# A two-block transformer kernel on Trainium2: the second norm summed per token, two query splits moved ahead, and the expert lists made between slabs 32 and 40

## The reference, cut to what matters

```python
h2 = modulate(x, norm2_g[l], shift2, scale2)          # rms_norm(x) * g * (1 + scale) + shift
q = (hf @ w_q).reshape(t, 8, 256)                     # PEER: 8 heads
s1, s2 = q[..., :128] @ keys_1.T, q[..., 128:] @ keys_2.T
v1, i1 = top_k(s1, 16); v2, i2 = top_k(s2, 16)
sc, ci = top_k(all 256 sums v1 + v2, 16)              # 16 experts per head of 16384
gates = softmax(sc)
a = gelu(einsum('td,ted->te', hb, u_tab[eb]))
out = einsum('te,ted->td', gates * a, v_tab[eb])
```

## Time and profile before

| What | Value |
|---|---|
| median of 3 runs | 1734.45 us (1734.1 to 1734.72) |
| the profiled execution's own time | 1732.42 us |
| its span | 1730.7 us |
| TensorE busy | 1639.6 us, 95% of the span |
| VectorE busy | 1067.3 us, 62% |
| ScalarE busy | 851.8 us, 49% |
| GpSimd busy | 492.4 us, 28% |
| mean granted TensorE clock | 0.974 |
| second norm, queries | about 184 to 264 us |
| slabs 0 to 39 | 266 to 387 us |
| lists, first gated slab | 387 to 398 us |

### The profile page before, as it was taken

How to read it: one execution, slowest core, us unless ns; L and a number is a source line. 1 busy time by engine, 2 the same in 40 slices (tenths; PEclk the granted TensorE clock), 3 DMA queues, 4 the chain that set the end, 5 groups by cost and what they waited for, 6 DMA issues and landing times.

```text
span 1730.7 us, 33796 instructions
## 1 busy us (share of the span) xinstructions
PE 1639.6 (95%) x11134; PEld 1490.6 (86%) x11134; DVE 1067.3 (62%) x2463; ACT 851.8 (49%) x1806; POOL 492.4 (28%) x485
## 2 busy tenths in 40 slices
PE   6998599999999999999999999889999999899998
PEld 4778598999999999887788877779999988789997
DVE  5665479907777751455565555866555665765555
ACT  3433345654444444555555553455555535754554
POOL 3110597885666678200000002411000000410000
PEclk9997799999999999999999999899999999999999
DMA  8871244553444445555555554227555435045554
GB/s 336 292 251 66 99 158 147 182 181 113 144 135 144 134 151 182 188 188 190 193 194 187 191 192 152 70 77 265 182 182 182 149 107 183 13 159 176 188 186 154
DMA packets 81330, 288.19 MB, mean 167 GB/s; under 512 B 10144, under 2 KB 11472, under 8 KB 81136
## 3 DMA queue, kind: packets, MB, share of 16 engines
q1 hardware_dynamic: 71296, 253.11, 44.0%
q0 software_dynamic: 8640, 31.07, 4.9%
q10 hardware_dynamic: 1328, 3.15, 0.5%
HBM read 284.66 MB, written 2.62 MB: 166 GB/s over the span
## 4 chain that ended last, share of the span: by engine, by line
PE 82%; DVE 7%; POOL 5%; issue 3%; ACT 3%; DMA 1%; DVEq 0%; ACTq 0%; POOLq 0%; SPq 0%
PE pu L615 12%; PE pu L616 11%; PE pu L617 11%; PE pacc L672 8%; PE pacc L674 8%; PE pacc L673 8%; POOL ring_lo L397 3%; PE pu L583 3%; PE pu L595 2%; PE pacc L615 2%; PE pacc L617 2%; PE pacc L616 2%; PE pn L960 2%; PE pm L960 2%; PE pacc L732 1%
## 5 line engine op out<-in xcount | busy, mean ns | idle before, releaser
L390 ACT ACTIVATE ring_hi<-ring 128x512 fp32r<-128x512 f32 x896 | 515.0, 622 | 545.8 <-PE pu L617 304.9
L397 DVE TENSOR_TENSOR ring_lo<-ring,ring_hi 128x512 fp32r<-128x512 f32 x608 | 395.9, 693 | 329.0 <-ACT ring_hi L390 328.8
L615 PE MATMUL pu<-Xh,ring_hi 128*128 128x256 f32 x1472 | 433.1, 294 | 33.5 <-POOL ring_lo L397 19.4
L616 PE MATMUL pu<-Xl,ring_hi 128*128 128x256 f32 x1472 | 421.4, 286 | 0.0
L617 PE MATMUL pu<-Xh,ring_lo 128*128 128x256 f32 x1472 | 421.2, 286 | 0.0
L397 POOL TENSOR_TENSOR ring_lo<-ring,ring_hi 128x512 fp32r<-128x512 f32 x288 | 370.2, 1307 | 131.9 <-ACT ring_hi L390 113.6
L615 PEld LDWEIGHTS pu<-Xh,ring_hi 128*128 128x128 f32 x1472 | 287.2, 195 | 40.6 <-issue 32.8
L616 PEld LDWEIGHTS pu<-Xl,ring_hi 128*128 128x128 f32 x1472 | 287.7, 195 | 0.2
L617 PEld LDWEIGHTS pu<-Xh,ring_lo 128*128 128x128 f32 x1472 | 286.9, 195 | 0.0
L674 PE MATMUL pacc<-ring_lo,vh 128*128 128x512 f32 x512 | 200.6, 392 | 0.0
L672 PE MATMUL pacc<-ring_hi,vh 128*128 128x512 f32 x512 | 200.5, 392 | 0.0
(11 more groups left out here) (402 smaller groups left out, 2649.4 us busy)
## 6 DMA issues: line engine op xcount, KB each, us to landing
ring<-in_weights SPq DMA_DIRECT2D x480, 512.0 KB, 3.4
big<-in_ada POOLq DMA_DIRECT2D x40, 512.0 KB, 6.4
big<-in_w1k POOLq DMA_DIRECT2D x8, 512.0 KB, 8.9
bias_row<-big ACTq DMA_DIRECT2D x1, 1536.0 KB, 6.8
XT<-in_xT ACTq DMA_DIRECT2D x1, 1024.0 KB, 8.4
scr<-in_ada POOLq DMA_DIRECT2D x2, 512.0 KB, 12.4
tk<-in_ada POOLq DMA_DIRECT2D x2, 512.0 KB, 14.1
early_h<-in_ada POOLq DMA_DIRECT2D x2, 512.0 KB, 16.1
```

Of the source, the lines that this page charges most:

```text
L390: nc.scalar.activation(ring_hi[:, n % 2, half], ring[:, n % RING, half], ACT.Copy).then_inc(s["split_hi"], 1)
L397: api.tensor_tensor(ring_lo[:, n % RING, half], ring[:, n % RING, half], ring_hi[:, n % 2, half], ALU.subtract).then_inc(s[LOW[name][0]], 1)
L615: mm(out, ring_hi[:, n % 2, w], xh, start=start, stop=False, skip_group_check=True)
L616: mm(out, ring_hi[:, n % 2, w], xl, start=False, stop=False, skip_group_check=True)
```

## The change

Three edits, all in the first block.

1. **The second norm.** GpSimd no longer adds squares. TensorE multiplies each chunk's squares (as the stationary side, one 128x128 block per half of the tokens) by one column of ones, so the sums come out with tokens on partitions, two columns in all. The sums of chunks 0 to 3 come before `out_slot(7)`, those of 4 and 5 after it, those of 6 and 7 after the last squares. Root and reciprocal work on two columns, and two products with the identity (an operand that repeats one column) spread the inverse roots to a 128x256 tile in PSUM, which `h2_scale` reads.
2. **The first query splits.** GpSimd makes the low parts of query tiles 0 and 1 right after its nine memsets; the loop behind the wait for `ada_used` has tiles 2 to 15, with one of the 14 memsets after each.
3. **The lists.** The loop of ungated slabs ends at 32. Slabs 32 to 39 are written out: the exponent comes after slab 31, the transposes after slab 34 on TensorE, the copies after the gelu of slab 35 on ScalarE. VectorE gets a wait for slab 39's result before its first `combine`.

```diff
+LISTS_AT = 32
             for k in range(mid_lo, mid_hi, 4):
                 step(nc.gpsimd.memset(big[:, k:min(k + 4, mid_hi), :], 1.0))
-            pool.wait_ge(s["h2_sq"], 2)
-            h2sum = R[:, T:2 * T]
-            step(nc.gpsimd.tensor_tensor(h2sum, sq[:, 0, :], sq[:, 1, :], ALU.add))
-            for c in range(2, C - 2):
-                pool.wait_ge(s["h2_sq"], c + 1)
-                last = nc.gpsimd.tensor_tensor(h2sum, h2sum, sq[:, c, :], ALU.add)
-                if c < C - 3:
-                    step(last)
-            last.then_inc(s["h2_sum"], 1)
+            split_low(pool, nc.gpsimd, "peer_q", 0)
+            split_low(pool, nc.gpsimd, "peer_q", 1)
...
-            for i in range(2 * PH):
+            for i in range(2, 2 * PH):
                 split_low(pool, nc.gpsimd, "peer_q", i)
-                for lo, hi in parts[i::2 * PH]:
+                for lo, hi in parts[i - 2::2 * PH - 2]:
                     step(nc.gpsimd.memset(big[:, lo:hi, :], 1.0))
...
-            for i in range(2, 8):
+            def h2_sums(c):
+                for tt in range(TT):
+                    last = mm(paccf[:, tt * 512:tt * 512 + 1], sq[:, c, tt * P:(tt + 1) * P], ones[:, 0:1],
+                              start=(c == 0), stop=(c == C - 1), skip_group_check=True)
+                return last
+            for i in range(2, 7):
                 out_slot(i)
+            for c in range(4):
+                pe.wait_ge(s["h2_sq"], c + 1)
+                h2_sums(c)
+            out_slot(7)
+            for c in range(4, C - 2):
+                pe.wait_ge(s["h2_sq"], c + 1)
+                h2_sums(c)
+            pe.wait_ge(s["squares"], SQUARED["n2"])
+            h2_sums(C - 2)
+            h2_sums(C - 1).then_inc(s["sums"], 1)
             pe.wait_ge(s["normed"], NORM["gla"])
-            pe.wait_ge(s["h2_sum"], 1)
-            mm(pn[:, 0:T], ones[:, :], R[:, T:2 * T], start=True, stop=False)
-            pe.wait_ge(s["squares"], SQUARED["n2"])
-            mm(pn[:, 0:T], ones[:, :], sq[:, C - 2, :], start=False, stop=False)
-            mm(pn[:, 0:T], ones[:, :], sq[:, C - 1, :], start=False, stop=True).then_inc(s["sums"], 1)
+            pe.wait_ge(s["inverses"], 4)
+            for tt in range(TT):
+                last = mm(pn[:, tt * P:(tt + 1) * P], over_columns(R[:, tt:tt + 1]), ident[:, :], start=True, stop=True)
+            last.then_inc(s["spreads"], 1)
...
-            with pe.Fori(0, GATED_FROM // BODY) as g:
+            with pe.Fori(0, LISTS_AT // BODY) as g:
...
-            pe.wait_ge(s["lists_ready"], 1)
-            (six transposes, lists_psum)
+            for k in range(LISTS_AT, GATED_FROM):
+                up_slot("peer_u", k, USE["peer_u"] + k, None, 0)
+                if k == LISTS_AT + 2:
+                    pe.wait_ge(s["lists_ready"], 1)
+                    for tt in range(TT):
+                        for q in range(3):
+                            bank = (pm, pn)[tt]
+                            last = nc.tensor.transpose(bank[:, q * P:(q + 1) * P], tk[:, 1536 + (q * TT + tt) * P:
+                                                       1536 + (q * TT + tt + 1) * P], ident[:, :])
+                    last.then_inc(s["lists_psum"], 1)
...
-            root(NORM["n2"])
+            act.wait_ge(s["sums"], NORM["n2"])
+            f(R[:, 0:TT].rearrange("p (a b) -> p a b", b=1),
+              paccf[:, 0:TT * 512].rearrange("p (a b) -> p a b", b=512)[:, :, 0:1],
+              ACT.Sqrt, scale=1.0 / D, bias=eps[:, 0:1]).then_inc(s["roots"], 1)
...
-            act.wait_ge(s["lists_psum"], 1)
...
+            for k in range(LISTS_AT, GATED_FROM):
+                split_high(act, "peer_u", k + 2)
+                expert_tile(k)
+                if k == LISTS_AT + 3:
+                    act.wait_ge(s["lists_psum"], 1)
+                    for tt in range(TT):
+                        last = f(Rl[:, :, tt * P:(tt + 1) * P],
+                                 (pm, pn)[tt][:, 0:3 * P].rearrange("p (q t) -> p q t", q=3), ACT.Copy)
+                    last.then_inc(s["lists_copied"], 1)
...
-                v.scalar_tensor_tensor(HTf[:, c, :], XT[:, c, :], gain[:, 8 + c:9 + c], R[:, 0:T], ALU.mult, ALU.mult)\
+                v.scalar_tensor_tensor(HTf[:, c, :], XT[:, c, :], gain[:, 8 + c:9 + c], pn[:, 0:T], ALU.mult, ALU.mult)\
...
-            step(v.reciprocal(R[:, 0:T], R[:, 0:T]))
+            v.reciprocal(R[:, 0:TT], R[:, 0:TT]).then_inc(s["inverses"], 1)
+            dve.wait_ge(s["spreads"], 4)
...
+            dve.wait_ge(s["evacs"], USE["peer_u"] + GATED_FROM)
             with dve.Fori(GATED_FROM // BODY, (GATED_FROM + GROUPS) // BODY - 1) as g:
```

More of the change, by code:

```diff
@@ L118 @@
 NSA_OUT = OUTNO[SPAN["nsa"][0]]
-SEMS = """c_loaded x_loaded cols_loaded relb_loaded small_loaded xn_ready h_scaled h_chunks h2_sq h2_sum h2_scaled h2_hi h2_lo consts_made casts_made c_silu ada_used chain_dve chain_act chain_pool slots_used evacs alr_psum
+SEMS = """c_loaded x_loaded cols_loaded relb_loaded small_loaded xn_ready h_scaled h_chunks h2_sq h2_scaled h2_hi h2_lo consts_made casts_made c_silu ada_used chain_dve chain_act chain_pool slots_used evacs alr_psum
 alr_copied z_psum squares sums roots normed la_parts ex_ready ex_done silu_done gla_ops kl_psum kl_copied gla_scores
@@ L1477, in _ @@
             split_high(act, "peer_u", 1)
-            with act.Fori(0, GATED_FROM // BODY) as g:
+            with act.Fori(0, LISTS_AT // BODY) as g:
                 for k in range(BODY):
```

## The result

The changed kernel takes **1715.78 us** (median of 4 runs, 1715.42 to 1716.95), against 1734.3 for the kernel before beside it (1734.1 to 1734.72): a ratio of 0.9894, 95% interval 0.9877 to 0.9911. The forecast was 1716.8, in a range of 1712 to 1723. The profiled execution took 1715.42 us, with a span of 1713.5.

What follows compares the result with a forecast made beforehand. The prediction took TensorE to bound the kernel, so only its waits or lower-clock time could pay. 11.1 us at the queries (norm included) plus 6.6 at the lists gave 17.7, from 1734.45 to 1716.8, range 1712 to 1723.

Steps and rivals of the forecast that it cites:

- The norm: Second norm: first scaling at 189.9 instead of 193.46, 3.6 us earlier, or 2.2 if both TensorE steps are slow.
- The first queries: Query tiles: first query at 191.4 instead of 206.59, but tile 15 gains only 11.1 us, paced by GpSimd's 3.48-us rounds.
- Rival 1, the half clock: Query tiles: TensorE stays at 1.2 GHz beyond tile 1, each tile taking 2.7 us more; chance 0.08 mild, 0.03 full.
- mild: Half clock for two query tiles: 5.4 us less 2.1 of slack, 1720.1; chance 0.08.
- full: Half clock for all 14 query tiles: tile 15 starts 33.0 us after the forecast, 1752 in all; chance 0.03.
- The sign that I had named: Query tiles: the granted clock at 0.5 past 204 would show the forecast wrong.
- the slack: Query tiles: TensorE has 13 x 0.16 = 2.1 us to spare, into which a slow clock may fall.
- Rival 2, GpSimd's pace: Query rounds: GpSimd's rounds shrink below TensorE's 3.32, tile 15 gains 4.5 us more, 1712.3; chance 0.06.
- Rival 4: First block: something else holds the first queries, leaving only 6.6 and 3.6 us of gain, 1724.3; chance 0.04.
- The lists: Slabs 32 to 40: removing the stop gives 7.2 us, less 0.6 for the transposes, a gain of 6.6.
- rival 3: Slab 32: ScalarE's table loads, exponent and copies reach TensorE through the splits, 4.0 us back, 1720.8; chance 0.09.
- The sum: Whole kernel: 11.1 + 6.6 = 17.7 us gain, median 1716.8, profiled execution 1714.7.

Runs made afterwards that it cites:

- e3: The changed kernel with the query splits and memsets of the kernel before, so the new norm alone: 2.86 us earlier at the scaling, 3.07 at tile 15.
- e9: The changed kernel with ScalarE's high parts of the first two slabs moved into the last two query rounds: first gated product 3.41 us earlier.
- e10: The changed kernel with nine unread identity products in TensorE's gaps around the norm: scaling 0.68 us earlier, time 1720.8 us.
- e4: The kernel before, with its own norm, and two query splits moved behind GpSimd's sum of squares: tile 15 7.55 us earlier.
- e7: The changed kernel with 13 of 14 memsets ahead of GpSimd's third split and the last behind all splits: tile 15 0.44 us earlier.
- e8: The changed kernel with the lists eight slabs earlier, at slab 24 instead of 32: first gated product 2.88 us later.
- e1: The kernel before with the edit of the lists alone: first gated product 6.99 us earlier.
- e6: The changed kernel with GpSimd's splits no longer waiting for the modulation products: 1.51 us earlier at tile 15, 2.73 at the first gated product.
- e12: The changed kernel with e10's products, rearranged memsets, splits not waiting for modulation, early slab splits, and tile 15's evacuation before the second slab's split: about 1710.91 us, intervals overlapping.

## Why the prediction was right

**The norm: right in kind, 0.7 too large.** I took 3.6 "as TensorE idles under 1 us at a time here"; measured are 2.89 at the scaling in the change and 2.86 in e3. The step that failed is the clock: it fell during the last sums, and the spread took 1.20 where I had 0.7, the last sums 1.21. The two prices named (3.6 at the full clock, 2.2 with both slow) hold it between them. e9 and e10 show the cause: with the clock up the same norm gives 3.58 and 3.57. Scaling from PSUM cost nothing, as forecast: two chunks take 0.87 us where they took 0.88.

**The first queries: right.** I said that only the 3.6 us would reach GpSimd's third split, and 7.5 more come from the splits moved away (11.1 less 3.6). Measured: 7.55 in e4. The third split started 21.28 us behind residual 6 where it had been 24.20, so it inherited the norm's 2.9. GpSimd's round of 3.48 held to the digit, and e7 shows that it was the bound: without memsets in it the tiles follow at 3.32. The total at tile 15 is 10.5 for 11.1, the difference being the norm's.

**Rival 1, the half clock: ruled out, though not idle.** The clock was back by 199, with the first matmuls of query 1, and I had let it rise in query 0 or tile 1. The rule of the Trainium skill's "TensorE: Matmul & The Clock Gate", section "A second HAM failure mode: psum-queue depth-cycling", that frequent short idles make the clock swing at a cost, agrees with this trace in kind (0.50 from 189 to 197, with pauses of 0.65 to 1.73 us). Its cost was 0.7 us, not the 3.3 (mild) or 35 (full) of the rival. The sign that I had named, 0.5 past 204, did show in seven of the experiments, behind the wait for the third split. In six of them the slack, which I had put at 2.1 us, took it up (e8: tile 15 at 67.89 as in the change); e7 had done away with it.

**Rival 2, GpSimd's pace:** it held in the change; e7 made it go and gained 0.4 of the 2.0, the clock taking the rest. **Rival 4** did not come: tile 15 starts 10.5 us earlier.

**The lists: 6.6 forecast, 7.0 measured** (e1 6.99). The transposes cost what I had: the slab with them took 3.52 us between two splits, 0.64 over 2.88. ScalarE's load, exponent and copies stayed hidden but for one wait of 0.2 us of TensorE at a slab, so rival 3 did not come; e8 shows that such a wait does come through when the exponent is asked for ahead of the logits. VectorE's division took 1.40 instead of 0.42, beside a GpSimd split, and was covered by the slabs ahead of the transposes. The other 0.4 us are a term of the sum: I let slab 40 start "some 0.2 us after 386.68", behind the end of slab 39's last matmul. In the kernel before that matmul starts at 386.37:

```profile
386.37 0.28 PE L617 MATMUL pu<-Xh,ring_lo 128*128 128x256 f32 x1
```

At this clock the matmuls of these slabs start 0.12 us apart and overlap, so slab 40 would have started at 386.49 and its products 2.88 later, at 389.37. That is 7.67 before 397.04; less the 0.64 of the transposes it is 7.0.

**The sum: 17.7 forecast, 17.44 measured** at the first gated product; two errors, 0.6 too much at the front and 0.4 too little at the lists, nearly cancel. In times it was 18.5 (1734.3 less 1715.78), in the two profiled executions 17.0 (1732.42 less 1715.42). The 1.0 us between the forecast of 1716.8 and the measured 1715.78 has another source: I put the median 2.0 above the profiled execution, as in the kernel before, and in the changed kernel it lies 0.36 above. The profiled execution was forecast at 1714.7 and took 1715.42, a miss the other way. That the two partly cancel is luck.

## What to carry to other kernels

Moving work off the engine that sets a pace gains only what its round loses: ask what else is in the round (here the memsets), and what the first item of the chain still waits for. After every wait that an edit moves or leaves on TensorE, count the clock behind it as well: 1.1 to 1.5 us for a wait of about 2 us here, in most executions and not in all, and nothing where TensorE has that much slack behind the wait (e8). And look for the same pattern at the next seam: the stop between query tile 15 and slab 0 stood in both kernels, and taking it away was worth 2.7 us.

## What the runs showed of the hardware

- **The clock behind a wait is not settled by its length.** A wait of 1.84 us (the change, tile 2) left the granted clock at 1.00, one of 1.93 at the same place (e7) was followed by 0.50; one of 2.34 was followed by 0.50 in the change and by 1.00 in e6. Even the same code does both: behind the wait at tile 2 the clock stayed up in the change and fell in e8 (1.82 us), and at the norm it fell in the change and stayed up in e9 until behind the spread. With the added products it stayed up in e10 and fell in e12. In all it fell behind 18 of the 20 waits of 1.8 to 2.4 us at tile 2, at slab 0 and, in e8, at the lists. What decides isn't shown.
- **VectorE and GpSimd slow each other.** A modulation product of VectorE went from 1.22 to 2.31 us and GpSimd's split from 2.50 to 3.80 when they met (e6); the division of 256 columns went from 0.42 to 1.40 beside a split. Memsets of GpSimd beside the same modulation products left them at 1.22 (e7). The Trainium skill's "GPSIMD Engine Reference", section "8. Key points", says that GpSimd contends for its SBUF interfaces with VectorE instructions that read two SBUF inputs; both of these do, and the trace agrees.
